# First mixer operands loaded and rotated a stage earlier; four attention tiles carried over the merge's stage boundary

## The reference, cut to what matters

```python
u = rms_norm(x, norm_mix_pre_w)
z, xbc, dt_raw, q, k, v, gate_ssd, gate_attn = _split(u @ w_in, IN_SIZES)
xbc = jax.nn.silu(causal_dwconv(xbc, ssd_conv_w, ssd_conv_b))
...
y = ssd_chunked(xh, dt, a, bm, cm)
y = y + ssd_d[..., None] * xh
y = gated_group_rms_norm(y, z, ssd_norm_w)
y_ssd = y @ ssd_w_out
q, k = apply_rope(q, cos, sin), apply_rope(k, cos, sin)
y_attn = sliding_window_sink_attention(q, k, v, attn_sinks) @ attn_w_out
merged = jax.nn.sigmoid(gate_ssd) * y_ssd + jax.nn.sigmoid(gate_attn) * y_attn
x = x + rms_norm(merged @ w_mix_out, norm_mix_post_w)
h = rms_norm(x, norm_ffn_pre_w)
up = causal_dwconv(h @ ffn_w_up, ffn_conv_w, ffn_conv_b)
gate, val = _split(up, (FFN_D_FF, FFN_D_FF))
return x + rms_norm((jax.nn.gelu(gate, approximate=True) * val) @ ffn_w_down, norm_ffn_post_w)
```

## Time and profile before

| | us |
|---|---|
| median of 3 runs | 2153.46 (2152.41 to 2155.26) |
| profiled execution: time | 2155.0 |
| profiled execution: span of the trace | 2153.4 |
| TensorE busy in it | 2065.3 (96%) |
| DVE, ACT, POOL busy | 1246.8, 890.8, 595.7 |

### The profile page before, as it was taken

One profiled execution on the slowest core, in us unless ns is written; L12 is line 12 of the kernel. 1 busy time (PEld: TensorE's weight loads), 2 busy tenths in 40 slices (PEclk: granted clock), 3 DMA queues, 4 the chain that ended last, 5 costly groups with the idle time before them and its releaser, 6 DMA issues. The chain is left out here.

```text
span 2153.4 us, 28476 instructions
## 1 busy us (share of the span) xinstructions
PE 2065.3 (96%) x9914; PEld 1684.3 (78%) x9914; DVE 1246.8 (58%) x1792; ACT 890.8 (41%) x1717; POOL 595.7 (28%) x600
## 2 busy tenths in 40 slices
PE   7999999979999989999969999999999999999997
PEld 6888889967767767767748888887888888878885
DVE  6854543226656656666643344568877777753523
ACT  5332221115565556555543222445443444443432
POOL 1000011145576666675510000015222222100000
PEclk9999999989999999999979999999999999999998
DMA  6223251224443443343264334321222212445342
GB/s 222 66 90 97 78 177 66 76 93 134 122 129 114 123 142 112 114 135 115 78 207 155 139 137 147 129 88 60 88 88 88 79 68 87 159 147 196 117 145 87
DMA packets 131262, 252.70 MB, mean 117 GB/s; under 512 B 25264, under 2 KB 70448, under 8 KB 131152
## 3 DMA queue, kind: packets, MB, share of 16 engines
q1 hardware_dynamic: 85584, 174.98, 25.5%
q0 software_dynamic: 15360, 55.32, 7.5%
q10 hardware_dynamic: 30208, 20.98, 3.0%
HBM read 189.63 MB, written 61.60 MB: 117 GB/s over the span
## 5 line engine op out<-in xcount | busy, mean ns | idle before, releaser
L155 PE MATMUL ps_zg<-u_hi,g_hi 128*128 128x512 f32 x448 | 185.9, 415 | 2.4 <-issue 2.4
L157 PE MATMUL ps_zg<-u_hi,g_lo 128*128 128x512 f32 x448 | 176.8, 395 | 0.0
L156 PE MATMUL ps_zg<-u_lo,g_hi 128*128 128x512 f32 x448 | 176.1, 393 | 0.0
L2043 DVE TENSOR_TENSOR lt_d_lo<-lt_w_raw,lt_d_hi 128x640 fp32r<-128x640 f32 (+1 forms) x64 | 57.1, 892 | 148.8 <-ACT lt_d_hi L1768 144.4
L155 PE MATMUL lt_ps<-lt_h_hi,lt_w_hi 128*128 128x512 f32 x256 | 100.5, 392 | 15.9 <-DVE lt_h_lo L2081 14.7
L155 PE MATMUL ps_zg<-z_w,u_hi 128*128 128x512 f32 x256 | 105.2, 411 | 2.0 <-POOL z_w L981 1.6
L974 POOL TENSOR_TENSOR mx_seg<-mx_seg,mx_cbm 128x1024 f32<-128x1024 f32 x32 | 76.4, 2386 | 109.3 <-ACT mx_seg L1038 109.3
L1768 ACT ACTIVATE lt_d_hi<-lt_w_raw 128x640 fp32r<-128x640 f32 (+1 forms) x64 | 50.8, 794 | 131.7 <-PE lt_ps L157 116.0
L1642 POOL TENSOR_TENSOR lt_t_f<-lt_w_raw 128x512 f32<-128x512 f32 x21 | 29.1, 1387 | 261.7 <-DVE lt_t_lo L1971 260.2
L157 PE MATMUL ps_zg<-z_w,u_lo 128*128 128x512 f32 x256 | 100.7, 393 | 0.0
L156 PE MATMUL ps_zg<-z_w,u_hi 128*128 128x512 f32 x256 | 100.4, 392 | 0.0
(11 more groups left out here) (389 smaller groups left out, 6112.7 us busy)
## 6 DMA issues: line engine op xcount, KB each, us to landing
lt_w_raw<-in_w_up SPq DMA_DIRECT2D x44, 512.0 KB, 4.5
mx_a_row<-acs_s SPq DMA_DIRECT2D x32, 512.0 KB, 3.9
g_raw<-in_w_xbc SPq DMA_DIRECT2D x24, 512.0 KB, 3.7
lt_sig<-gate_s SPq DMA_DIRECT2D x24, 512.0 KB, 3.6
lt_w_raw<-in_w_down SPq DMA_DIRECT2D x32, 384.0 KB, 3.2
ff_s<-lt_fo SPq DMA_DIRECT2D x21, 512.0 KB, 5.2
tok_s<-fr_work POOLq DMA_DIRECT2D x20, 512.0 KB, 4.0
lt_w_raw<-in_w_down SPq DMA_DIRECT2D x32, 320.0 KB, 2.9
```

What stands on the lines that cost most here:

```text
L155: pe.matmul(dst, s_hi, m_hi, start=first, stop=False)
L156: pe.matmul(dst, s_hi, m_lo, start=False, stop=False)
L157: return pe.matmul(dst, s_lo, m_hi, start=False, stop=last)
L2043: dve.tensor_tensor(d_lo[:, m % 2, 0:n], w_raw[:, m % 2, 0:n], d_hi[:, m % 2, 0:n].bitcast(F32), ALU.subtract).then_inc(dw_lo_done, 1)
```

## The change

1. **Operands of steps 0 and 1.** The tiles of `load_step` move into `Carry` (`work` and `held` share the place of front tiles), and SP issues both steps' loads inside front: the parts that don't need the last rows between z pieces 1 and 2, and q, k, v between the z pieces after row tiles 0 and 1 are stored. POOL rotates q and k of step 0 in front (`rotate_first`) between two row stores, into a part of `carry.raw`. ACT's table load moves to front too. z pieces lie at another place in `carry.raw`.
2. **Groups written out.** The `Fori` over groups 1 and 2 is a Python loop on all five engines.
3. **The change of groups reordered.** SP loads `z_late` one step earlier. ACT copies and stores the gate block before it splits `z_late`, where it did so after the exponentials. DVE splits k 4 to 6, makes `rden`, and then splits k 7 and scales the carried state.
4. **Merge begun in mixers.** The first four attention tiles are loaded by SP in the last step into `o_raw` and split by ACT and DVE into `z_w`, whose z weights are used up; two more (`next_raw`) are loaded but not split. The weights of blocks 0 and 1 take the place of gate weights (`g_hi[:, 0]` and `out_hi`) in the last group, and add a split to ACT and DVE in steps 6 and 7 of it. PE makes block 0's four products `merge(0)` to `merge(3)` in `carry.ps` around the last transposes and values. In late PE starts with block 1's four, then sources 4 to 7 for both. Sources 12 to 15 lie in `z_w` too, so they are split only when block 7 has used the first four tiles (`o_used`).

Cut to its core (line numbers left out; `load_step` and the moved tile declarations cut):

```diff
@@ front, SP @@
-            for q in range(4):
+            for q in range(2):
                 load_z(q)
+            sp.wait_ge(acs_stored, 16)
+            for j in range(2):
+                sp.wait_ge(t_stored[j], 16 * token_pairs)
+                sp.wait_ge(f_stored[j], 16 * (n_pairs - feature_pairs))
+            for c in range(2):
+                for dst, src in (
...
+                    (carry.x_in[:, c], tok_s[c, :, 0:GW]),
...
+                ):
+                    sp.dma_start(dst, src).then_inc(carry.step_in[c], 16)
...
+            for c in range(2):
+                sp.wait_ge(stored[c], 16 * ((RC - 1) * NT // OR + 1))
+                for dst, src in (
+                    (carry.qk[:, c, 0:REP].rearrange("p a d -> p (a d)"), rows_s[c, :, Q0:Q0 + REP * HD]),
...
+                ):
+                    sp.dma_start(dst, src).then_inc(carry.step_in[c], 16)
+                load_z(2 + c)
@@ front, POOL @@
+            def rotate_first():
...
+                pool.wait_ge(carry.step_in[0], 16 * 8)
+                pool.wait_ge(rw_lo_done, 2 * RC)
+                pool.wait_ge(exps_done, 2)
...
+                pool.tensor_tensor(carry.qr[:, :, HD // 2:HD], carry.m1, carry.m2, ALU.add).then_inc(carry.rotated, 1)
...
                     store_rows(c, t)
+                    if c == RC - 1 and t == 3:
+                        rotate_first()
@@ front, ACT @@
+            act.preload_act_table_set("natural_log_exp_and_others")
             act.wait_ge(carry.g_in[0], 16)
@@ mixers, SP @@
-                    if c == NT - 1 and not last:
+                    if c == NT - 2 and not last:
                         sp.wait_ge(z_done, NT * g + NT)
                         for q in range(2, 4):
                             load_z(g + 1, q)
...
+                    if last and c == NT - 1:
+                        sp.wait_ge(z_done, NG * NT)
...
+                        for k in range(EARLY):
+                            sp.dma_start(carry.o_raw[:, k], o_s[k]).then_inc(o_in[k], 16)
+                        sp.wait_ge(gate_done, NG * NT)
...
+                            sp.dma_start(carry.next_raw[k][:], o_s[EARLY + k]).then_inc(next_in, 16)
+                        sp.wait_ge(next_in, 16 * RAW)
@@ mixers, every engine @@
             group(0, True, False)
-            with pe.Fori(1, NG - 1) as g:
+            for g in range(1, NG - 1):
                 group(g, False, False)
             group(NG - 1, False, True)
@@ mixers, ACT, a step @@
                     if not opening:
                         outputs(g if c else g - 1, (c - 1) % NT, first and c <= 2, range(4) if change else ())
+                    ending = last and c == NT - 1
+                    if ending:
+                        split_o(0)
+                    if change or ending:
+                        gate_tile(g, c, first)
                     if change:
                         for k in range(4, KT):
                             split_z(g + 1, k)
...
+                    if not (change or ending):
+                        gate_tile(g, c, first)
...
                     ins.then_inc(p_scaled, 1)
+                    if ending:
+                        split_o(1)
+                        split_o(2)
@@ mixers, DVE, a step @@
-                    if c == NT - 1 and not last:
-                        for k in range(4, KT):
+                    change = c == NT - 1 and not last
+                    if change:
+                        for k in range(4, KT - 1):
                             split_z(g + 1, k)
...
                     dve.reciprocal(rden[:], rden[:]).then_inc(rden_ready, 1)
+                    if change:
+                        split_z(g + 1, KT - 1)
+                        carried_y()
@@ mixers, PE @@
                     next_z(g, c, last_group, range(KT))
+                    if last_group and c == NT - 1:
+                        merge(0)
                     pe.wait_ge(p_scaled, n + 1)
...
             group(NG - 1, False, True)
+            merge(1)
             values(NG - 1, NT - 1)
+            merge(2)
             turn_outputs(NG - 1, NT - 1, False)
+            merge(3)
@@ late, POOL @@
-            for n in range(MERGE):
-                if n >= 3:
-                    pool.wait_ge(s_lo_done, n - 2)
-                pool.dma_start(y_t[:, n % 3], o_s[n] if n < KT else y_s[n - KT]).then_inc(s_in[n % 3], 16)
+            for m in range(RING):
+                n = m + EARLY + RAW
+                if m >= 3:
+                    pool.wait_ge(s_lo_done, m + RAW - 2)
+                pool.dma_start(y_t[:, m % 3], o_s[n] if n < KT else y_s[n - KT]).then_inc(s_in[m % 3], 16)
@@ late, PE @@
-            for k in range(KT):
+            for k in range(EARLY):
+                for h in range(2):
+                    merge(1, k, h)
+            for k in range(EARLY, KT):
                 for n in range(2):
-                    if k == 0:
-                        pe.wait_ge(w_lo_done, n + 1)
                     if n == 0:
-                        pe.wait_ge(s_lo_done, k + 1)
+                        pe.wait_ge(s_lo_done, k - EARLY + 1)
```

302 lines of the change are left out of this document (215 added, 87 removed).

## The result

The changed kernel takes 2118.7 us, median of four runs (2117.05 to 2119.47). The kernel before, run beside it, takes 2153.99 us. The ratio is 0.9838, with a 95% interval of 0.9826 to 0.9851: faster by 1.6%, 35.3 us. The forecast was 2116.4 us with a range of 2109 to 2127.

The account below looks back on a forecast made before the run. PE, busy 96% of 2153.4 us, was taken as the bound, so time comes only from its idle and half-speed stretches. 10.6 + 12.2 + 14.3 = 37.1 us off the 2153.46 us median gave 2116.4 us, range 2109 to 2127.

Parts of the forecast that it names:

- First border: Border of front and mixers: POOL's copies and the `diag` matmuls start earlier, saving 10.6 us (9.5 to 11.6).
- a possible gain of 1 us: First border: a further 1 us if half clock after 474.35 does not come.
- Changes of groups: Three group changes: PE's waits, the stop on "issue" and half clock go, saving 12.2 us (7 to 13).
- The waits on the weights: Three group changes: PE's waits ahead of the transposes of attention weights close, saving 6.8 us.
- DVE makes it at 768.5, PE wants it at 769.0: Second group change: DVE's split of k 7 behind `rden` is estimated ready just before PE needs it.
- no wait over 0.5 us: Sign for the group changes: no PE wait on the transposes longer than 0.5 us.
- the port rival: Group changes: the port DVE shares with POOL holds up `rden`, about 1 us each, 3 in all; no separate chance.
- The stop at the loop's end: Second group change: PE's stop on "issue" lies at the loop's branch back; writing groups out saves 2.4 us.
- The rival that it belongs to something else: Second group change: the stop is not the branch's and stays with its half clock, 2120.9 us; chance 0.06.
- The half clock that was to go with it: Behind the second change's stop: half clock disappears with the idle time, 1.8 us of the 3.0 us clock term.
- The slower case: Groups 1 and 2: fetching written-out code stops PE in each of 16 steps, 67 us, 2183.6 us; chance 0.03.
- Mixers' end and merge: Mixers' end to block 2: merge begun early gains 16.3 us, less 2.0 for a later border: 14.3 us (10 to 16).

Follow-up runs that it names:

- e5: Changed kernel with the first rotation of q and k back at the mixers' start, its loads still in front: 2120.9 us.
- e6: Changed kernel with the first two steps' loads and the first rotation of q and k back behind the border of front and mixers: 2129.4 us.
- e2: Changed kernel with the load of the last z pieces issued in a group's last step again, not one step earlier: 2127.3 us.
- e1: Changed kernel with groups 1 and 2 again one looped body on all five engines, nothing reordered: 2125.2 us.
- e9: Changed kernel with the loop over groups 1 and 2 back on PE alone: 2125.4 us.
- e7: Changed kernel with the merge's first 24 matmuls all behind the last step's operations, still ahead of the border: 2119.5 us.
- e8: Changed kernel with the merge's first 24 matmuls moved behind the border: 2123.1 us.
- e10: Changed kernel with ACT's attention output copy first in group changes and the very first step's skip product behind the mix: 2120.6 us.

## Why the prediction was right, and where only its sum was

**First border (10.6 us).** Right at its place: 10.62 at the `diag` matmuls, POOL the bound, front unaffected (e5, e6). 9.4 remained, just under the 9.5 of the range. What the term lacked is the clock behind them: I saw a possible gain of 1 us if half clock did not come, and it came for 6 us of work instead of 3.4, since a shorter wait ahead hides less of it.

**Changes of groups (12.2 us).** Measured 12.5, but by other terms. The waits on the weights went (6.8), and so did the stop (2.4), as said; 3.7 us of waits in the following steps, on ACT's copy of y above all, went too, which I had not counted. Against this the changed kernel has 3 x 0.71 + 3 x 0.98 = 5.1 us of new waits. All idle stretches of PE over 0.2 us from 600 to 1075 us of the kernel before add up to 14.6 us, and of the changed kernel, without the last step's, to 6.9: 7.7 us, where 9.2 was predicted. Of the other 4.8 us the granted clock accounts for 3.8, where 3.0 was predicted: it was 0.50 from 772.93 to 779.76 us, with PE busy for 4.46 of them, and from 929.95 to 933.36, with PE busy for 3.12; half of the busy time is lost. I had priced it in full at the second change and only in the transposes at the third. The last 1.0 us I can't place. The step "DVE makes it at 768.5, PE wants it at 769.0" was a margin of 0.5 us between two estimates, and it missed by 1.2. The condition "no wait over 0.5 us" held for the transposes, not for the z product ahead of them. Of the 1.2 us, 0.37 are the sum for `rden`, which took 0.55 us where it was 0.18 in e2 and 0.20 in the kernel before: 1.1 us in three changes, where the port rival had up to 3. POOL's rotation ran beside it in all three kernels, and each time the sum ended within 0.02 us of the end of POOL's instruction (755.90 and 755.88 us in the changed kernel, 760.19 and 760.17 in e2, 769.69 and 769.67 before). That speaks for the shared port, and for its length being set by where in POOL's instruction it falls.

**The stop at the loop's end (2.4 us).** Right, and shown by e1 and e9. The rival that it belongs to something else is out. The half clock that was to go with it is not the stop's alone: e1 and e9 have a longer stop and stayed at full clock behind it. The slower case is out too: 16 written-out steps show not one stop on "issue".

**Mixers' end and merge (14.3 us).** Measured 15.1. From the border to block 2 it is 18.3 us, where 18.2 was predicted. The border came 1.0 us late, not 2.0: the store stands 15.0 us behind the last `diag` matmuls, 14.0 before. e7 and e8 show that PE's 24 matmuls have no part in that. That leaves ACT and DVE, whose added splits, and ACT's gate copy put further ahead, were in both of these runs; taking out either alone was not tried. No new wait stands in blocks 0 to 9.

**The total.** 37.1 predicted, 37.0 at block 2, 37.9 in the profiled span, 35.3 between the medians. So the 2.3 us that the forecast misses are not in the three terms. 0.5 of them are the kernel before, which took 2153.99 us beside the changed one and not 2153.46. 1.2 can be put to the last stores of the output, which land that much later behind the last matmul in every trace of the new code; the prediction put the part behind the merge at nothing. Why they land later is not shown. The remaining 0.6 are within what executions of one kernel differ by, and the forecast could not have had them: it is worked out from one profiled execution, 1.5 us above its median, and the changed kernel's lies 1.6 below its own.

## What to carry to other kernels

Where two chains meet in one operation, the costs of undoing either must not be added: here 6.6 and 7.4 us became 9.2 together, and by the same figures moving one chain alone would have brought 1.8 or 2.6 us of the 9.2. A wait that is removed ahead of another wait on the same engine gives back only what the later one does not take: e10 removed three waits of 1.0 us and gained nothing. And a loop's way back on a saturated engine costs microseconds, so few long iterations may be better written out.
